# Three-part short-format products for the first projections, convolutions read from their banks, earlier turns of query and key rows

## The reference

```python
h = modulate(rms_norm(x, norm_mix[l]), shift1, scale1)
proj = h @ w_in[l]
(g_q, g_k, g_v, g_z, g_a, g_b, s_q, s_k, s_v) = jnp.split(proj, split_points, axis=-1)
gdn_out = gated_deltanet(g_q, g_k, g_v, g_z, g_a, g_b, ...)
swa_out = sliding_window_attention(s_q, s_k, s_v, q_norm[l], k_norm[l], sinks[l], positions)
```

## Time and profile before

| what | value |
|---|---|
| median of 3 runs | 2470.33 us (2466.88 to 2471.84) |
| profiled execution | 2469.46 us, of which its span is 2467.6 us |
| busy share of the span | PE 94%, PEld 76%, DVE 35%, ACT 27%, POOL 26% |
| mean granted PE clock | 0.964 |
| instructions | 30933 |

### The profile page before, as it was taken

How to read it: one execution, slowest core, us unless ns; L and a number is a source line. 1 busy time by engine, 2 the same in 40 slices (tenths; PEclk the granted TensorE clock), 3 DMA queues, 4 the chain that set the end, 5 groups by cost and what they waited for, 6 DMA issues and landing times.

```text
span 2467.6 us, 30933 instructions
## 1 busy us (share of the span) xinstructions
PE 2331.7 (94%) x12323; PEld 1885.6 (76%) x12324; DVE 862.0 (35%) x1356; ACT 655.1 (27%) x1008; POOL 644.9 (26%) x264
## 2 busy tenths in 40 slices
PE   7998889989789999989999998999999998999998
PEld 5644458877679999968887876888865876888787
DVE  4165744444511111151333014232734634322302
ACT  2023323443210000042222123333335324222212
POOL 0023013422100000014434333324413342343432
PEclk7998889999899999999999999999999998999999
DMA  9121510002148888712233223223322322323222
GB/s 298 52 86 51 167 73 1 1 1 79 61 134 292 299 294 290 248 52 86 89 98 99 86 89 104 86 77 112 103 77 94 103 86 85 103 85 102 86 86 94
DMA packets 220360, 278.00 MB, mean 113 GB/s; under 512 B 9704, under 2 KB 199108, under 8 KB 220261
## 3 DMA queue, kind: packets, MB, share of 16 engines
q1 hardware_dynamic: 211744, 267.49, 32.9%
q10 hardware_dynamic: 7140, 4.87, 0.7%
q0 software_dynamic: 1376, 4.26, 0.5%
HBM read 272.36 MB, written 4.24 MB: 112 GB/s over the span
## 4 chain that ended last, share of the span: by engine, by line
PE 87%; DVE 5%; ACT 3%; issue 1%; DMA 1%; DVEq 1%; ACTq 1%; POOL 0%; POOLq 0%
PE bank L2431 47%; PE bank L2067 10%; PE bank L2075 5%; PE bank L615 3%; PE bank L583 2%; PE bank L1515 2%; PE bank L446 1%; PE bank L1823 1%; PE bank L3215 1%; PE bank L1508 1%; PE bank L3234 1%; DMA ring<-in_ffn_w_down 1%; PE bank L603 1%; PE bank L406 1%; PE bank L2858 1%
## 5 line engine op out<-in xcount | busy, mean ns | idle before, releaser
L2431 PE MATMUL bank<-hT_high_split,ring_split 128*128 128x512 f32 x2496 | 797.5, 399 | 4.2 <-DVEq L2545 3.0
L2431 PEld LDWEIGHTS bank<-hT_high_split,ring_split 128*128 128x128 f32 x2496 | 471.3, 189 | 116.1 <-DVEq L2545 3.8
L2431 PE MATMUL bank<-hT_split,ring_split 128*128 128x512 f32 x1248 | 491.7, 394 | 0.0
L2415 POOL TENSOR_TENSOR ring_split<-ring,ring_split 128x2048 fp32r<-128x2048 f32 x60 | 277.4, 4625 | 425.7 <-ACT ring_split L2400 425.7
L2400 ACT ACTIVATE ring_split<-ring 128x2048 fp32r<-128x2048 f32 x108 | 206.9, 1916 | 649.1 <-DMA ring<-in_ffn_w_down 196.1
L2431 PE MATMUL bank<-ring_split,hid_high_split 128*128 128x512 f32 x848 | 272.8, 402 | 10.7 <-DVE hid_low_split L2555 7.3
L2431 PEld LDWEIGHTS bank<-hT_split,ring_split 128*128 128x128 f32 x1248 | 236.0, 189 | 57.2 <-issue 0.2
L2771 POOL TENSOR_TENSOR ring_split<-ring,ring_split 128x2048 fp32r<-128x2048 f32 x40 | 186.0, 4650 | 332.9 <-ACT ring_split L2400 332.8
L2067 PE MATMUL bank<-arena,ring 128*128 x2048 | 236.4, 277 | 5.1 <-issue 5.1
L2067 PEld LDWEIGHTS bank<-arena,ring 128*128 128x128 f32 x2048 | 233.7, 194 | 5.3 <-issue 5.3
L2431 PEld LDWEIGHTS bank<-ring_split,hid_high_split 128*128 128x128 f32 x848 | 161.6, 191 | 51.8 <-DVE hid_low_split L2555 8.2
(11 more groups left out here) (470 smaller groups left out, 2745.5 us busy)
## 6 DMA issues: line engine op xcount, KB each, us to landing
ring<-in_w_in SPq DMA_DIRECT2D x45, 1024.0 KB, 5.1
ring<-in_w_gate SPq DMA_DIRECT2D x32, 1024.0 KB, 5.5
ring<-in_w_up SPq DMA_DIRECT2D x32, 1024.0 KB, 8.0
ring<-in_w_down SPq DMA_DIRECT2D x32, 1024.0 KB, 7.4
ring<-in_ffn_w_gate SPq DMA_DIRECT2D x22, 1024.0 KB, 5.3
ring<-in_ffn_w_up SPq DMA_DIRECT2D x22, 1024.0 KB, 5.3
ring<-in_ffn_w_down SPq DMA_DIRECT2D x22, 1024.0 KB, 4.9
ring<-in_w_ada SPq DMA_DIRECT2D x16, 1024.0 KB, 5.2
```

What stands on the lines that cost most here:

```text
L2415: pool.tensor_tensor(low(n), raw(n), high(n).bitcast(F32), ALU.subtract)\
L2431: mm = pe.matmul(dst, left[l], right[r], start=start and n == 0, stop=stop and n == 2)
```

## The change

- **Three-part products.** All five products of the first projections are made as `three`. The weights are split in the ring: ACT writes the high part of each slot to free memory (`act_p1`), and the low part goes back in place (`p1_low`), by DVE for slots 0, 1, 9 and 10 and by POOL for slots 2 to 8. `hT` is split likewise (`act_hT`, `dve_hT`). g_a and g_b join s_k and s_v: four products of 272, 256, 16 and 272 columns for each row block and k. The high parts of slots 9 and 10 lie in the ring places of slots 7 and 8, so SP loads slots 13 and later only after slot 10 is used.
- **Convolutions from their banks.** The twelve blocks use banks 6, 7, 0, 1 in turn. ACT does the last tap while it takes the bank, DVE adds the other three from the bank itself; there is no `convin`.
- **Turns.** g_q is turned after block m = 8 and g_k after m = 10, between the products, through banks 2 to 5; g_v after g_z. s_k is turned before s_q, and s_q's four copies follow one by one.
- **Factors.** The gain of s_q is multiplied into the tables of the rotation, and 1/rms times 64 ** -0.5 is the scalar of the mask step. POOL's eight multiplications of s_q and eight of s_k go away; DVE gets `dve_swa_prep` at m = 4. q * exp(G) moves from DVE to POOL.

```diff
+        P1 = list(range(FIRST["sq"], FIRST["z"] + 2))
...
-                    sp.wait_ge(S("slots_used"), i - RING + 1)
+                    free = i - RING + 1
+                    if (i - RING) in (P1[7], P1[8]):
+                        free = P1[-1] + 1
+                    sp.wait_ge(S("slots_used"), free)
...
+        def act_hT(act, scale, shift):
+
+            nxt(act, "mod_ready")
+            for k in range(KD):
+                nxt(act, "x_turned")
+                if k % 2 == 0:
+                    act.activation(hT[:, k, :], bank[k][:, :], ACT.Identity, bias=shift[:, k:k + 1],
                                    scale=scale[:, k:k + 1])
-            tally[(str(act.engine), "x_turned")] += 1
-            i.then_inc(S("hT_even"), 1)
+                    act.drain()
+                    act.activation(h_hi[:, k, :], hT[:, k, :], ACT.Copy).then_inc(S("h_high"), 1)
+                else:
+                    act.activation(h_hi[:, k, :], bank[k][:, :], ACT.Identity, bias=shift[:, k:k + 1],
+                                   scale=scale[:, k:k + 1]).then_inc(S("h_high"), 1)
...
+        def dve_hT(dve, scale, shift):
+            for k in range(KD):
+                nxt(dve, "h_high")
+                if k % 2:
+                    nxt(dve, "x_turned", 2)
+                    dve.tensor_scalar(hT[:, k, :], bank[k][:, :], scale[:, k:k + 1], shift[:, k:k + 1],
                                       ALU.mult, ALU.add)
-            i.then_inc(S("hT_odd"), 1)
+                    dve.drain()
+                dve.tensor_tensor(h_lo[:, k, :], hT[:, k, :], h_hi[:, k, :].bitcast(F32), ALU.subtract)\
+                   .then_inc(S("h_low"), 1)
...
+        def act_p1(act, s):
+
             n = SLOTS[s].shape[-1]
...
+            act.wait_ge(loaded[s % RING], 16 * (s // RING + 1))
+            if s >= Z:
+                act.wait_ge(S("slots_used"), P1[7 + s - Z] + 1)
+            elif s - 1 >= 4:
+                old = s - 4 if s - 5 >= SKV else s - 5
+                act.wait_ge(S("slots_used"), old + 1)
+            if s == SKV:
+                nxt(act, "wab_loaded", 16)
+                act.activation(skv_hi[:, :, 256:272], wab, ACT.Copy)
+            act.activation(p1_hi(s, n), slot_view(s, n), ACT.Copy).then_inc(S("p1_high"), 1)
+
+        def p1_low(e, s, done):
+            n = SLOTS[s].shape[-1]
+            e.wait_ge(S("p1_high"), s + 1 + before("p1_high"))
+            w = slot_view(s, n)
+            parts = 1 if done == "p1_low_dve" else 4
+            k = w.shape[1] // parts
+            for q in range(parts):
+                c = slice(q * k, q * k + k)
+                i = e.tensor_tensor(p1_lo(s, n)[:, c, :], w[:, c, :], p1_hi(s, n)[:, c, :].bitcast(F32), ALU.subtract)
+            if s == SKV:
+                i = e.tensor_tensor(ab_lo, wab, skv_hi[:, :, 256:272].bitcast(F32), ALU.subtract)
+            i.then_inc(S(done), 1)
+
+        def need_low(pe, s):
+            nxt(pe, "p1_low_dve" if s < SKV or s >= Z else "p1_low_pool")
+
+        def pe_gemm_n(pe, s, banks, first=False):
 
             for half in range(2):
-                need(pe, s + half)
...
+                need_low(pe, s + half)
+                w = (p1_hi(s + half, 512), p1_lo(s + half, 512))
+                for i in range(4):
+                    k = 4 * half + i
+                    if first and k == 0:
+                        nxt(pe, "h_low", 4)
+                    elif first and k >= 4:
+                        nxt(pe, "h_low")
+                    for t in range(NT):
+                        c = slice(t * P, (t + 1) * P)
+                        mm = three(pe, banks[t][:, :], (h_hi[:, k, c], h_lo[:, k, c]), [x[:, i, :] for x in w],
+                                   k == 0, k == KD - 1)
...
+            pe_gemm_n(pe, FIRST["sq"], bank[0:4], True)
...
+                c, b = slice(t * P, (t + 1) * P), bank[2 + t]
                 for k in range(KD):
...
+                    pe.matmul(b[:, 0:272], h_hi[:, k, c], skv_hi[:, k, :], start=(k == 0), stop=False)
+                    pe.matmul(b[:, 0:256], h_hi[:, k, c], lo[:, k, :], start=False, stop=False)
+                    pe.matmul(b[:, 256:272], h_hi[:, k, c], ab_lo[:, k, :], start=False, stop=False)
+                    mm = pe.matmul(b[:, 0:272], h_lo[:, k, c], skv_hi[:, k, :], start=False, stop=(k == KD - 1))
...
+                    m = 2 * i + j
+                    if m >= 4:
+                        nxt(pe, "conv_done")
                     for k in range(KD):
-                        mm = pe.matmul(bank[j][:, :], w[:, k, j * P:(j + 1) * P], hT[:, k, :],
-                                       start=(k == 0), stop=(k == KD - 1))
+                        mm = three(pe, bank[CONV_BANKS[m % 4]][:, :], [x[:, k, j * P:(j + 1) * P] for x in w],
+                                   (h_hi[:, k, :], h_lo[:, k, :]), k == 0, k == KD - 1)
...
+                    if m == 8:
+                        nxt(pe, "skv_taken")
+                        pe_qkv(pe, 0, (2, 3, 4, 5))
+                    if m == 10:
+                        nxt(pe, "qkv_taken", NT)
+                        pe_qkv(pe, 1, (2, 3, 4, 5))
+            nxt(pe, "conv_done")
...
+                if m >= 4:
+                    nxt(act, "silu_done")
+                act.activation(convacc[:, m % 4, :], bank[CONV_BANKS[m % 4]][:, :], ACT.Identity, bias=con("zero"),
+                               scale=cols1[:, at + 36 + m:at + 37 + m]).then_inc(S("conv_in"), 1)
+                if j == 0 and i < 4:
+                    act_p1(act, FIRST["qkv"] + i + 2)
+                if m == NM - 3:
+                    act_p1(act, Z)
+                if m == NM - 1:
+                    act_p1(act, Z + 1)
...
-            dve.tensor_scalar(convacc[:, j, :], convin[:, j, 3:3 + T], cols1[:, at + 36 + m:at + 37 + m],
-                              None, ALU.mult)
             for tap in range(3):
-                dve.drain()
+                d = 3 - tap
                 w = cols1[:, at + 12 * tap + m:at + 12 * tap + m + 1]
-                i = dve.scalar_tensor_tensor(convacc[:, j, :], convin[:, j, tap:tap + T], w,
-                                             convacc[:, j, :], ALU.mult, ALU.add)
+                i = dve.scalar_tensor_tensor(acc[:, d:T], src[:, 0:T - d], w, acc[:, d:T], ALU.mult, ALU.add)
+                if tap < 2:
+                    dve.drain()
...
+                if m == 3:
                     dve_gdn_gate(dve)
-                if m == 6:
-                    nxt(dve, "w_normed")
-                    nxt(dve, "rotation")
-                if 6 <= m < 6 + NT:
+                if m == 4:
+                    dve_swa_prep(dve)
+                if 6 <= m < 9:
                     dve_rope(dve, m - 6)
-            dve.drain().then_inc(S("w_qk"), 1)
+                if m == 9:
+                    p1_low(dve, Z, "p1_low_dve")
+                if m == 10:
+                    dve_rope(dve, NT - 1)
+                    dve.drain().then_inc(S("w_qk"), 1)
+            p1_low(dve, Z + 1, "p1_low_dve")
...
+        def dve_swa_prep(dve):
+
+            nxt(dve, "w_roots")
+            dve.reciprocal(w_ss, w_r)
+            nxt(dve, "rotation")
+            half = HD // 2
+            shape = [P, NT, half]
+            norm = row("q_norm")
+            for x, c, n in ((rope_c1, cos, 0), (rope_s2, sin, half), (rope_s1, sin, 0), (rope_c2, cos, half)):
+                dve.tensor_tensor(x, c, norm[:, n:n + half].unsqueeze(1).broadcast_to(shape), ALU.mult)
+            dve.drain()
+            dve.tensor_scalar(w_ss[:, :, 0:H], w_ss[:, :, 0:H], HD ** -0.5, None, ALU.mult)
             for t in range(NT):
-                k4 = sk3[:, t, :].rearrange("p (h e) -> p h e", e=HD)
-                pool.tensor_tensor(sq4[:, t], sq4[:, t], w_ss[:, t, 0:H].unsqueeze(2).broadcast_to([P, H, HD]), ALU.mult)
-                pool.tensor_tensor(k4, k4, w_ss[:, t, H:NW].unsqueeze(2).broadcast_to([P, 2, HD]), ALU.mult)
-            nxt(pool, "rows_loaded", 16 * len(ROWS))
-            pool.drain()
-            for t in range(NT):
-                k4 = sk3[:, t, :].rearrange("p (h e) -> p h e", e=HD)
-                pool.tensor_tensor(sq4[:, t], sq4[:, t], row("q_norm").unsqueeze(1).broadcast_to([P, H, HD]), ALU.mult)
-                i = pool.tensor_tensor(k4, k4, row("k_norm").unsqueeze(1).broadcast_to([P, 2, HD]), ALU.mult)
-            i.then_inc(S("w_normed"), 1)
+                for g in range(2):
+                    k = sk3[:, t, HD * g:HD * g + HD]
+                    dve.scalar_tensor_tensor(k, k, w_ss[:, t, H + g:H + g + 1], row("k_norm"), ALU.mult, ALU.mult)
+            dve.drain()
...
-            for j in range(NPAIR):
-                for t in range(NT):
-                    pe.transpose(bank[j][:, t * P:(t + 1) * P], sq[:, t, j * P:(j + 1) * P], ident)
             for g in range(2):
                 for t in range(NT):
-                    mm = pe.transpose(bank[4 + g][:, t * P:(t + 1) * P],
```

(31 more changed lines are left out.)

209 lines of the change are left out of this document (96 added, 113 removed).

## The result

The changed kernel takes 2442.76 us (median of four runs, 2441.5 to 2443.43), the kernel before 2470.46 beside it: a ratio of 0.989, 95% interval 0.9872 to 0.9907. That is 27.7 us faster, where the prediction had 39.0 us and 2431.3 us. The measurement lies 0.2 us inside the upper end of the stated range (2423 to 2443) and outside that of outcome A (2425 to 2438). The profiled execution took 2443.43 us and has a span of 2441.6 us.

The account below looks back on a forecast made before the run. PE, 87% of the span, was taken as the bound. 40.5 us gained up to the first scores less 1.5 us given back made 39.0 us, from the median 2470.33 to 2431.3 us; range 2423 to 2443.

Parts of the forecast that it names:

- outcome A: The main forecast, all terms as summed: 2431 us, own range 2425 to 2438; chance 0.60.
- rival C: Three-part records on PE go faster than 0.2325 us, at 0.215: 8.4 us less, 2423 us; chance 0.06.
- step 2: s_q: 32 products at 0.70 us plus 2.3 for starting behind a wait, 24.7 us, ending at 83.9; -5.2 us.
- Rival D: The combined product of s_k, s_v, g_a and g_b runs at its upper end: +10.5 us, 2442 us; chance 0.09.
- rival E: Slower than before: later weight slots load only after g_z, so seven pairs wait 6 us each, 2473 us; chance 0.02.
- step 1: Start of s_q, behind the splits of slots 0 and 1 and of hT: 59.2 instead of 55.63 us, +3.6.
- What is given back: POOL's 20 scalings run beside the first four attention units and slow DVE there: 1.5 us lost, between 0 and 7.5.
- If all doubled: Upper bound of the attention loss: DVE's 14 two-input sums beside POOL all take twice as long, 7.5 us.
- PE is the fuller engine there, so I take 1.5.: First attention units: PE busy 22.25 of 24 us, DVE 17.09, so DVE's slowdown beside POOL costs only 1.5 us.
- Rival B: DVE and POOL in each other's way, DVE's two-input operations doubling beside POOL: 31 us gained, 2440 us; chance 0.20.
- the rotations: Slowed by POOL, they put g_z's first low part 10 us later, to 176.5: 1.3 us of wait.
- step 7: From g_z to the scores: copies of g_z, then s_k's and s_q's turns; scores at 203.6, 2.1 us less gain at half clock.

Follow-up runs that it names:

- e1: Changed kernel with POOL's 20 scalings left out, four of the five arrays set to a constant instead; 2428.76 us, ratio 0.9827.
- e4: Changed kernel with the mask step's factor a constant instead of the column with the row's norm; 2441.76 us, ratio 0.9878.
- e5: Kernel before, with POOL's 16 scalings held back by one more wait so that they lie beside the first attention units; 2482.91 us, ratio 1.0039.
- e2: Changed kernel with each of POOL's 20 scalings of 512 columns cut into four of 128; 2435.49 us, ratio 0.9852.

## Why the prediction was off

**The steps to the scores were right.** By the earlier trace rows and the rows above:

| step | forecast | measured |
|---|---|---|
| start of s_q | 59.2 | 58.98 |
| s_q | 24.7 | 25.2 (86.78 - 2.65 - 58.98) |
| wait for the copies of s_q | 2.7 | 2.65 |
| combined product | 16.2 | 17.1 (103.85 - 86.78) |
| twelve blocks with turns | 71.4 | 70.3 (174.16 - 103.85) |
| g_z | 22.4 | 22.2 (197.14 - 174.97) |
| PE's first scores | 203.6 | 202.71 |
| gain there, from 244.08 | 40.5 | 41.4 |

The first mask step gains 40.7 us and not 41.4, since the last copy of s_q ends at 204.05. Three-part records start 0.23 us apart at the full clock, 0.2325 in the earlier trace rows, which closes rival C. The first 5.7 us of s_q ran at the lower clock, with 0.43 us from record to record. That is the start that step 2 of the prediction carried over from before at 2.3 us. The combined product takes 0.48 us a set where 0.505 was forecast; the 17.1 us hold a stretch from 88.6 to 92 us at the lower clock (0.58 in the window), behind PE's wait. Rival D is closed. Turns ran at the full clock (window 198 to 202), no low part of a weight was late, and the loads of rival E had landed in time: PE has no idle time ahead of line 451. (In step 1, 53.2 + 4.2 and DVE's 1.5 for k = 3 make 58.9 and not 59.2, which is nearer to the 58.98 measured.)

**The step that failed is "What is given back".** It had the right place, the right engines and the right row, and sized the term at 1.5 us with 7.5 as its upper bound. It measured 11.4 us in the attention. Three things in it were wrong:

- "If all doubled" read the earlier trace rows as a factor: 14 sums of 0.485 us at 1.45 / 0.686 give the 7.5 us. DVE's 1.45 us there is as near to one POOL instruction (median 1.233 us) and a little, and the experiments bear that out. As a wait for POOL's instruction it is much the same for any size, so 256 columns went to 1.16 us and not to 0.97 or 1.03.
- Only the 14 two-input sums of the earlier trace rows were counted. Seven of them met POOL and cost 4.4 us. Lines 1021 and 1023 on two columns and line 486 with one array pay as well: eight instructions, up to 1.1 us each, 5.7 us in all (the second of line 486 waits at the same time as line 1023). Those of lines 1021 and 1023 stand between the scores and the exponentials, where PE waits.
- "PE is the fuller engine there, so I take 1.5." The window gives 22.25 of 24 us to PE, but 17.09 us of DVE in 24 leave it 1 us in a unit of 3.5, and units 0 and 1 put 4.2 us more on it each (2.4 and 1.6 ahead of line 489, 1.9 and 2.6 in it), so DVE became the bound (21.96 us busy of 24).

Rival B named the two engines and the place, with the same factor of two, and was given 0.20. Its 2440 us come close to the 2442.76 measured in part by luck. Its terms are 7.5 us here, 1.3 us at the rotations and, "with a lower clock in step 7", 2.1 us more; off 40.5 they leave 31.7 without the clock and 29.6 with it, and the text has 31. The first term was 11.4, and the two others were nothing: the rotations were hit (1.51 us instead of 0.42 beside POOL's low part at 147 us), but it was hidden, and step 7 had the full clock. Off the 40.7 us, 11.4 leave the 29.3 of the meeting.

**The last microsecond of the 11.4.** From the mask step of unit 4 the changed kernel takes 79.4 us to the meeting, before 78.4 and e1 77.7, with no POOL work in any; e4 excludes the mask step. The rows of PE, changed and then before, show where it goes:

```profile
225.54 5.11 PE L451 MATMUL bank<-ring,cact 128*1 128x256 f32 x16
```

```profile
256.45 3.61 PE L446 MATMUL bank<-ring,cact 128*1 128x256 f32 x16
```

PE had waited 2.84 us for ACT just before and ran at a granted clock of 0.56 from 225.5 to 229 us (1.00 from 256.4 to 260 before). So the group ended 2.24 us behind the mask step of unit 4 instead of 1.30 (0.75 in e1), and from its end on the three kernels take 77.2, 77.1 and 76.9 us. In all ten traces in which POOL is done by then, units 4 and 5 take 11.8 us and that lag. So 0.9 of this 1.0 us is the trail of POOL's delay in the units before, by way of PE's clock; this is read from the traces, and no run tested it by itself.

**What stays open.** Why the stretch behind the meeting varies by more than 3 us from execution to execution (2130.5 in before and 2134.2 us in e5, which run the same instructions there).

## What to carry to other kernels

Before moving POOL work, list what DVE does beside it and sort it by operands: in these traces instructions with arrays in SBUF alone pay up to one POOL instruction each, whatever their size (and once 8 us), while the mask step, which reads a bank, and the reduction pay nothing. Then ask whether those instructions stand in a chain that PE waits for; a busy share of PE in the window does not answer that. Here the overlap could be moved away, by the order of POOL's work and by giving part of it to ACT. Where it can't, tiny DVE instructions are poor company for long POOL instructions: six of two columns, 1 us of work in all, cost 4.8 us.

## What was not expected of the hardware

- A DVE instruction on 128x2 elements stood for 8.23 us beside a run of POOL instructions of 0.40 us, in unit 0 of e2's profiled execution.
- POOL's product with a constant takes longer than the one with a broadcast column (1.48 against 1.04 to 1.08 us for 128x512) and is far less in DVE's way.
- A memset of POOL holds up line 1023 (one input, two columns) as well: it took 1.28 us instead of 0.17 in unit 2 of the changed kernel, until 222.9 us, where the memsets end.
- A column as scalar adds 0.06 us to a mask step that reads a bank, and nothing to the time.
